# Loading the first expert's first two weight chunks before the expert stage, with bf16 bias rows and a bf16 scatter in three parts

## The chip, the cores and the metric

The kernel runs as one program on one core of a Trainium2 chip. The metric is the device time of one execution in microseconds (us); the time before is 3459.2 us, the median of 3 runs (3454.86 to 3460.97). A lower time is better. Everything is computed in float32 unless bf16 is named.

## What is computed

The input is 256 tokens of width 1024. A first block runs attention, a mixture of 32 experts with 4 chosen for each token, and layer norms; a second block of two layers follows (chunked MLP, gated linear attention, and a lookup of single rows in two large tables, called PEER). Cut to what matters here:

```
def first_block(x, ...):
    y = layer_norm(ALPHA * x + token_mixer(x, w_in, sinks, w_proj_a, w_proj_b, w_out))
    logits = y @ router_w + router_b            # 32 experts
    top_val, top_idx = top_k(logits, 4)
    gates = softmax(top_val)
    for each token and each chosen expert e:
        g = min(y @ w_gate[e] + b_gate[e], 7.0)
        u = clip(y @ w_up[e] + b_up[e], -7.0, 7.0)
        h = g * sigmoid(1.702 * g) * (u + 1.0)
        out += gate * (h @ w_down[e] + b_down[e])
    return layer_norm(ALPHA * y + out)
```

The weights of one expert are three 1024 by 1024 matrices, 12.6 MB, and all 32 experts are read. The second block also has context tokens (`ctx`, 256 by 1024, 1 MB) that are worked on beside the experts.

## The kernel before

**Memory.** Weights come through a ring in SBUF: `sb_ring`, 6 slots of 128 x 4096 floats, 2 MB each. `Ring.load` (issued by L154 from SyncE, here SP) sends one DMA for each chunk of a fixed list, in order, and ahead of each DMA it waits until the slot's former chunk is used up (`chunk_used`). TensorE (PE) waits for a chunk with `Ring.wait` and gives the slot back with `Ring.used`. `sb_arena` is scratch of 16384 columns that is cut anew for each stage; `sb_X` and `sb_H` hold 4 rows of 1024 columns each.

**Front (0 to 316 us).** Attention, the output projection (`w_out`), layer norm and the router. The modulation vectors of the second block are made beside it from 24 chunks `w_mod`. Chunk order at its end: `w_proj_a`, `w_proj_b` x2, `w_out` x2, the last four `w_mod`, then expert 0's chunks `moe0.0` to `moe0.5`. The router's loads (`Router.begin`) and the context tokens (`sb_X<-in_ctx`) go out after the attention; the expert biases (`Router.rest`) go out after the layer norm (`y_ready`). All engines meet at a barrier before the expert stage, and SP comes to it only when these have landed (`Router.loaded`).

**Expert stage (316 to 1315 us).** `expert(p, e)` on PE, for expert e: four short matmuls that put the bias rows into PSUM (L1637, both halves of the columns, gate and up), then `halves` for chunks 0 to 3 (gate and up, L1607), the gather of tokens for a later expert (L1584), transposes of h (L1653), the scatter of the *former* expert's result to the tokens (L1598, `acc[..] += weighT x ye`), the transposes of the weights (L1660), any context work due at this expert (`beside.upto(e)`), and `halves` for chunks 4 and 5 (down projection). `e.c` names chunk c of expert e. VectorE (DVE) makes g, u and h, and ScalarE (ACT) the sigmoid and the copies out of PSUM. Eight chunks for the context work (`context0` to `context7`) stand in the same list, so the ring carries 200 chunks in this stage. SP's order sets the order of all loads: in the stage it runs

```
context.begin(sp)
...
for e in range(NE):
    ring.load(sp, ring.at[f"moe{e}.{PER_EXPERT - 1}"] + 1)
    context.sync(sp, e)
```

Right behind the stage GpSimd (POOL) starts to gather rows of the PEER tables by DMA.

## Time and profile before

| what | value |
|---|---|
| median of 3 runs | 3459.2 us |
| the profiled execution's own time | 3464.24 us |
| its span in the trace | 3462.4 us |
| PE busy, share of the span | 91% |
| DVE, ACT, POOL busy | 54%, 33%, 26% |
| mean DMA rate over the span | 395 GB/s |
| granted TensorE clock, mean | 0.984 |

The profiled execution is 5.0 us above the median. "Busy" is the time in which an engine has an instruction running; for PE the ends of pipelined matmuls are modelled. The DMA rate in slices of 86.6 us shows where transfers are dense and where they pause. Times in rows count from the start of the span.

### The profile page before, as it was taken

What the parts mean: (1) busy time and instruction counts of PE and PEld (TensorE: products, weight loads), DVE (VectorE), ACT (ScalarE), POOL (GpSimd) and SP (SyncE); (2) the same over time, 40 slices, a digit from 0 to 9 for tenths busy, and PEclk for the clock granted to TensorE, in tenths of its full rate; (3) what the DMA queues carried; (4) which work ended last, traced back from release to release, by engine and by line L of the source; (5) the groups of instructions that cost most, each with busy time, mean ns of one, the idle gap of its engine ahead of it and who ended that gap; (6) DMA issues with size and microseconds to landing.
All of it is one profiled execution on the core that took longest, in us unless ns stands there. A gap on an engine that the chain in (4) does not pass through costs nothing. (4 is left out here: it accounts for less than half of the span.)

```text
span 3462.4 us, 33187 instructions
## 1 busy us (share of the span) xinstructions
PE 3144.8 (91%) x10968; PEld 1409.5 (41%) x10968; DVE 1867.1 (54%) x4131; ACT 1131.4 (33%) x3028; POOL 885.8 (26%) x800
## 2 busy tenths in 40 slices
PE   8999999999999997999999888889888998987777
PEld 7574333433334432443345323333332643532222
DVE  7765102111221126776676677667765378667665
ACT  1331111110111113444344444555333434444333
POOL 0000000000000003443444444444442034444332
PEclk9999999999999999999999999999999999999999
DMA  9838999999999999999999999999998479999997
GB/s 404 366 136 341 426 427 428 426 425 428 419 427 428 415 428 405 403 421 414 389 421 416 417 421 419 408 418 412 418 421 343 168 302 420 421 420 421 421 413 329
DMA packets 155665, 1366.42 MB, mean 395 GB/s; under 512 B 18365, under 2 KB 18877, under 8 KB 24162
## 3 DMA queue, kind: packets, MB, share of 16 engines
q0 software_dynamic: 111360, 805.46, 56.4%
q1 hardware_dynamic: 44130, 558.80, 38.7%
q8 instruction: 89, 1.46, 0.2%
q14 instruction: 86, 0.70, 0.1%
HBM read 1363.04 MB, written 1.15 MB: 394 GB/s over the span
## 5 line engine op out<-in xcount | busy, mean ns | idle before, releaser
L3459 PE MATMUL ps<-sb_arena,sb_diag 128*128 128x512 f32 x3072 | 1474.3, 619 | 263.7 <-ACT sb_diag L3438 261.3
L1946 POOL DMA_INDIRECT sb_arena<-in_uv,sb_idx x768 | 865.7, 1127 | 2158.3 <-PE ps L3459 1046.5
L3394 DVE SCALAR_TENSOR_TENSOR sb_arena<-sb_arena,sb_H 128x1024 f32<-128x1024 f32 x768 | 941.1, 1226 | 586.7 <-DMA sb_arena<-in_uv,sb_idx 399.2
L3459 PEld LDWEIGHTS ps<-sb_arena,sb_diag 128*128 128x128 f32 x3072 | 562.6, 194 | 1122.5 <-ACT sb_diag L3438 562.1
L1607 PE MATMUL ps<-sb_ring,sb_arena 128*64 128x512 f32 x3072 | 675.1, 594 | 7.3 <-DMA sb_ring<-in_moe 7.3
L3427 ACT ACTIVATE sb_act<-sb_dots 128x1 f32<-128x1 f32 x768 | 154.8, 202 | 990.7 <-DVE sb_arena L3394 985.5
L1607 PEld LDWEIGHTS ps<-sb_ring,sb_arena 128*64 128x64 f32 x3072 | 214.2, 137 | 446.7 <-issue 430.8
L1808 DVE TENSOR_SCALAR sb_arena<-ps 128x512 f32<-128x512 f32 x32 | 22.1, 692 | 587.1 <-PE ps L1607 571.8
L3438 ACT ACTIVATE sb_diag<-sb_consts,sb_act 128x128 f32<-128x128 f32 x768 | 308.4, 402 | 38.9 <-PE ps L3459 14.1
L3433 ACT ACTIVATE sb_act<-sb_act,sb_wts 128x1 f32<-128x1 f32 x768 | 226.2, 295 | 24.9
L185 PE MATMUL ps<-sb_ring,sb_arena 128*128 128x512 f32 x256 | 111.6, 593 | 2.2 <-DVE sb_arena L889 1.6
L1815 DVE TENSOR_SCALAR sb_arena<-ps 128x512 f32<-128x512 f32 x32 | 22.1, 692 | 158.1 <-PE ps L1607 158.1
L1724 ACT ACTIVATE sb_arena<-sb_arena 128x512 f32<-128x512 f32 x32 | 20.2, 630 | 251.0 <-DVE sb_arena L1808 251.0
L1718 ACT ACTIVATE sb_arena<-ps 128x512 f32<-128x512 f32 x32 | 19.1, 598 | 234.0 <-PE ps L1584 234.0
L1741 ACT ACTIVATE sb_arena<-ps 128x512 f32<-128x512 f32 x32 | 19.1, 598 | 226.9 <-PE ps L1607 226.9
L425 POOL DMA_DIRECT2D mod_rows<-sb_arena x24 | 12.5, 527 | 307.7 <-ACTq L411 307.7
L349 DVE SCALAR_TENSOR_TENSOR sb_arena<-sb_ring,sb_wts,sb_arena 128x2048 f32<-128x2048 f32 x38 | 87.5, 2348 | 1.4 <-DVE sb_arena L349 1.1
L2596 PE MATMUL ps<-sb_ring 128*128 128x512 f32 x192 | 87.7, 600 | 0.0
L185 PE MATMUL ps<-sb_arena,sb_ring 128*128 128x256 f32 x352 | 76.9, 379 | 0.6 <-issue 0.5
L185 PEld LDWEIGHTS ps<-sb_ring,sb_arena 128*128 128x128 f32 x256 | 47.9, 190 | 61.2 <-issue 58.0
L1584 PEld LDWEIGHTS ps<-sb_arena,sb_X 128*128 128x128 f32 x512 | 59.6, 191 | 27.1 <-issue 24.3
L185 PEld LDWEIGHTS ps<-sb_arena,sb_ring 128*128 128x128 f32 x352 | 66.5, 190 | 10.1 <-issue 1.2
(447 smaller groups left out, 2599.0 us busy)
## 6 DMA issues: line engine op xcount, KB each, us to landing
sb_ring<-in_moe SPq DMA_DIRECT2D x192, 2048.0 KB, 16.9
sb_ring<-in_w_mod SPq DMA_DIRECT2D x24, 2048.0 KB, 14.3
sb_ring<-in_w_in SPq DMA_DIRECT2D x10, 2048.0 KB, 14.0
sb_ring<-in_a_w_in SPq DMA_DIRECT2D x8, 2048.0 KB, 15.6
sb_ring<-in_w_q SPq DMA_DIRECT2D x6, 2048.0 KB, 13.0
sb_arena<-in_uv,sb_idx POOLq DMA_INDIRECT x768, 14.7
sb_ring<-in_b_w_in SPq DMA_DIRECT2D x6, 2048.0 KB, 8.8
sb_ring<-in_a_w_out SPq DMA_DIRECT2D x4, 2048.0 KB, 13.9
```

The costliest lines, as they stand in the source:

```text
L185: last = nc.tensor.matmul(out, lhs, rhs, start=i == 0, stop=i == len(pairs) - 1)
L349: ins = nc.vector.scalar_tensor_tensor(out=out, in0=w[:, k, :], scalar=scale, in1=out, op0=ALU.mult, op1=ALU.add)
L1584: last = nc.tensor.matmul(m.ps[:, 7, k * P:(k + 1) * P], m.X[:, t, c:c + P], x.both[:, t, :], start=t == 0, stop=t == TT - 1)
L1607: last = nc.tensor.matmul(m.ps[n * SLOTS:(n + 1) * SLOTS, bank, :], lhs(k + KT // 2 * (c % 2), n), w[:, k, n * 512:(n + 1) * 512], start=f ...
L1808: nc.vector.tensor_scalar(x.g, m.ps[:, 4, :], LIMIT, None, ALU.min).then_inc(M(name("g_ready", p)), 1)
L1946: pool.indirect_dma_start(row_buffer(m, n), None, d[f"uv{layer}"], bass.IndirectOffsetOnAxis(m.idx[:, pair % 2, k:k + 1], 0))\
L2596: last = nc.tensor.matmul(m.ps[:, where[0], :], lhs(k), w[:, k, :], start=k == 0, stop=k == KT - 1)
L3394: nc.vector.scalar_tensor_tensor(out=u, in0=u, scalar=1.0, in1=m.H[:, order[i], :], op0=ALU.mult, op1=ALU.mult, accum_out=m.dots[:, n_ % P ...
L3427: nc.scalar.activation(a, m.dots[:, n_ % PK:n_ % PK + 1], ACT.Gelu_apprx_tanh).then_inc(M("gelu_done"), 1)
L3433: nc.scalar.activation(a, a, ACT.Copy, scale=m.wts[:, pair % 2, k:k + 1]).then_inc(M("act_ready"), 1)
L3438: nc.scalar.activation(m.diag[n_ % DIAGS], m.const("ident"), ACT.Copy, scale=a).then_inc(M("diag_ready"), 1)
L3459: last = nc.tensor.matmul(out[h], m.diag[n_ % DIAGS], uv[b][:, D + h * 512:D + (h + 1) * 512], start=opens, stop=ends)
```

## The change

It has four parts.

1. `moe0.0` and `moe0.1` leave the ring. `first_chunk` loads `moe0.0` in two halves into `sb_H` (rows 0 and 1) and `sb_X` (rows 2 and 3), where the context tokens went; `second_chunk` loads `moe0.1` into the end of the arena (columns 12288 on) once the gates are merged (`merged_ready`). The other chunks keep their order; all slots are turned by two (`(n + 2) % NSLOT`).
2. The context tokens and the two modulation rows for them (`Context.begin`) are loaded in the expert stage, after SP has waited until chunk `moe0.2` is used up, and they stand ahead of the loads of expert 1. DVE waits for three loads (48) in place of two.
3. Gate and up biases are cut into three bf16 parts whose sum is the float32 value: ACT rounds (`bias_upper`, `bias_middle`), POOL subtracts (`bias_less`), and six small DMAs from SBUF to SBUF (`bias_rest`) stack the parts on 96 partitions. PE adds them with four bf16 matmuls of 96 rows in place of four float32 ones of 32 rows.
4. The scatter of all experts but the last uses bf16: DVE makes a 0/1 matrix (`mine`) and three bf16 parts of the result (`split`), ACT multiplies by the gate when it copies the result (`scale=x.gate`), and PE runs twelve bf16 matmuls (`scatter_parts`) in place of four float32 ones.

```
+            router.first_chunk(sp)
+            ring.load(sp, ring.at["w_out"] + 2)
+            sp.wait_ge(M("merged_ready"), KT)
+            router.bias_load(sp)
+            router.second_chunk(sp)
+            ring.load(sp, ring.at["moe0.2"] + 2)
             sp.wait_ge(M("y_ready"), 2 * TT)
             banks.wait_full(sp, mod.where[MOD_END])
             router.rest(sp)
-            ring.load(sp, ring.at["moe0.0"] + PER_EXPERT)
+            router.bias_rest(sp)
+            ring.load(sp, ring.at["moe0.2"] + PER_EXPERT - 2)
             router.loaded(sp)
...
     def begin(self, sp):
         d, M = self.d, self.M
+        self.ring.wait_used(sp, "moe0.2")
+        sp.dma_start(self.m.X[:, 2:4, :], d["ctx"].rearrange("(t p) c -> p t c", p=P)).then_inc(M("context_in"), 16)
...
-            context.begin(sp)
...
             for e in range(NE):
                 ring.load(sp, ring.at[f"moe{e}.{PER_EXPERT - 1}"] + 1)
+                if e == 0:
+                    context.begin(sp)
                 context.sync(sp, e)
...
+            def scatter_parts(count):
+                pe.wait_ge(M("parts_ready"), count)
+                for t in range(TT):
+                    for part in range(3):
+                        for n in range(2):
+                            rows = slice(n * SLOTS, (n + 1) * SLOTS)
+                            last = nc.tensor.matmul(acc[2 * t + n], x.mine[rows, t * P:(t + 1) * P], x.parts[rows, part, :],
...
+                for which in range(2):
+                    for n in range(2):
+                        nc.tensor.matmul(m.ps[n * SLOTS:(n + 1) * SLOTS, 4 + which, :], x.select[0:96, :],
+                                         x.biases[0:96, which, n * 512:(n + 1) * 512], start=True, stop=False, skip_group_check=True)
...
+            def split(e):
+                dve.wait_ge(M("added"), e + 2)
+                dve.wait_ge(M("weighT_ready"), e + 2)
+                step(nc.vector.tensor_scalar(x.mine, x.weighT, 0.0, None, ALU.is_gt))
+                dve.wait_ge(M("ye_ready"), e + 2)
+                step(nc.vector.tensor_copy(x.parts[:, 0, :], x.ye))
+                step(nc.vector.tensor_tensor(x.ye, x.ye, x.parts[:, 0, :], ALU.subtract))
+                step(nc.vector.tensor_copy(x.parts[:, 1, :], x.ye))
+                step(nc.vector.tensor_tensor(x.parts[:, 2, :], x.ye, x.parts[:, 1, :], ALU.subtract), "parts_ready")
```

SP's queue at the end of the front, before the change (in the ring, a slot's number stands in the wait `chunk_used`; here without waits):

```order
L154 DMA sb_ring<-in_w_proj_b 128x4096 x2
L968 DMA sb_H<-in_lns 128x1024 x2
L1358 DMA sb_arena<-in_router_w 128x256
L1358 DMA sb_arena<-in_router_b 1x32
L1359 DMA sb_X<-in_ctx 128x2x1024
L154 DMA sb_ring<-in_w_out 128x4096 x2
L154 DMA sb_ring<-in_w_mod 128x4096 x4
L154 DMA sb_ring<-in_moe 128x4096 x2
L1364 DMA sb_arena<-in_b_gate 32x1024
L1364 DMA sb_arena<-in_b_up 32x1024
L1364 DMA sb_arena<-in_b_down 32x1024
L154 DMA sb_ring<-in_moe 128x4096 x4
```

The same place after the change:

```order
L1390 DMA sb_H<-in_moe 128x2048
L1390 DMA sb_X<-in_moe 128x2048
L154 DMA sb_ring<-in_w_out 128x4096 x2
L1407 DMA sb_w_gate<-in_b_gate 32x1024
L1407 DMA sb_w_gate<-in_b_up 32x1024
L1383 DMA sb_arena<-in_moe 128x4096
L154 DMA sb_ring<-in_w_mod 128x4096 x4
L154 DMA sb_ring<-in_moe 128x4096 x2
L1394 DMA sb_arena<-in_b_down 32x1024
L1402 DMA sb_arena<-sb_arena 32x1024 x2
L1402 DMA sb_arena<-sb_spare 32x1024 x2
L1402 DMA sb_arena<-sb_arena 32x1024 x2
```

Behind these rows only two ring chunks (`moe0.4`, `moe0.5`) go out in the front, where there were four: the six chunks of expert 0 are then all sent, two of them outside the ring.

SP's queue at the start of the expert stage, before the change, with its waits (`ISA` rows clear semaphores):

```order
L1042 DMA sb_H<-mod_rows 128x1024 x2
L1043 DMA sb_stats<-in_a_b_s 128x8
L1044 DMA sb_late_keys<-in_keys 128x128
L1527 ISA x34
L1504 TENSOR_LOAD sb_count [waits late_count]
L1504 ISA x2
L154 DMA sb_ring<-in_moe 128x4096 [waits chunk_used4]
L154 DMA sb_ring<-in_moe 128x4096 [waits chunk_used5]
```

And after the change (`chunk_used0` ahead of the context tokens is the use of `moe0.2`):

```order
L1585 ISA x37
L1563 TENSOR_LOAD sb_count [waits late_count]
L1563 ISA x2
L1053 DMA sb_X<-in_ctx 128x2x1024 [waits chunk_used0]
L1055 DMA sb_H<-mod_rows 128x1024 x2
L1056 DMA sb_stats<-in_a_b_s 128x8
L1057 DMA sb_late_keys<-in_keys 128x128
L154 DMA sb_ring<-in_moe 128x4096 [waits chunk_used4]
L154 DMA sb_ring<-in_moe 128x4096 [waits chunk_used5]
```

What was issued at once now stands behind a wait for a chunk of expert 0, and the first loads of expert 1 stand behind it too; their own slots (4 and 5) are those of the last two `w_mod` chunks.

PE's rows in the middle of one expert, before the change (gather L1584, transposes of h L1653, scatter L1598, transposes of the weights L1660):

```order
L1584 MATMUL ps<-sb_arena,sb_X 128x128 [waits both_picked,bank_free7]
L1584 MATMUL ps<-sb_arena,sb_X 128x128 x7
L1653 MATMUL ps<-sb_consts,sb_arena 128x128 [waits ye_ready,h_ready]
L1653 MATMUL ps<-sb_consts,sb_arena 128x128 x3
L1598 MATMUL ps<-sb_arena 128x512 x4
L1660 MATMUL ps<-sb_consts,sb_arena 128x128 [waits weigh_ready]
L1660 MATMUL ps<-sb_consts,sb_arena 128x128
```

And after it (gather L1644, transposes L1731, scatter L1669, transposes L1738):

```order
L1644 MATMUL ps<-sb_arena,sb_X 128x128 [waits both_picked,bank_free7]
L1644 MATMUL ps<-sb_arena,sb_X 128x128 x7
L1731 MATMUL ps<-sb_consts,sb_arena 128x128 [waits ye_ready,h_ready]
L1731 MATMUL ps<-sb_consts,sb_arena 128x128 x3
L1669 MATMUL ps<-sb_arena 128x512 [waits parts_ready]
L1669 MATMUL ps<-sb_arena 128x512 x11
L1738 MATMUL ps<-sb_consts,sb_arena 128x128 [waits weigh_ready]
L1738 MATMUL ps<-sb_consts,sb_arena 128x128
```

The scatter has twelve matmuls and a wait of its own, for DVE's `split`; before, its four matmuls had none. The four bias matmuls ahead of chunk 0 stay four (L1637 before, L1715 after).

## Rows read from the trace of the kernel before

**Rows 1.** The page, DMA rate in 40 equal slices of the span

```profile
GB/s 404 366 136 341 426 427 428 426 425 428 419 427 428 415 428 405 403 421 414 389 421 416 417 421 419 408 418 412 418 421 343 168 302 420 421 420 421 421 413 329
```

**Rows 2.** Busy time by window: PE, PEld, DVE, ACT, POOL, clock, DMA share, GB/s

```profile
173.00:220.00 47.00, 44.88 (x262) 31.74 (x260) 28.07 (x98) 18.35 (x59) 0.00 (x0) 1.00 0.20 68
268.00:280.00 12.00, 11.39 (x26) 4.96 (x27) 10.76 (x7) 0.00 (x0) 0.00 (x0) 1.00 0.59 199
341.40:1305.10 963.70, 953.09 (x4602) 384.04 (x4602) 169.54 (x393) 126.11 (x209) 3.07 (x4) 1.00 1.00 425
1140.00:1220.00 80.00, 80.00 (x423) 32.09 (x417) 18.20 (x64) 10.09 (x18) 0.00 (x0) 1.00 1.00 418
```

**Rows 3.** Waits in the expert stage: total us, times, longest us

```profile
PE ps L1607 <- DMA sb_ring<-in_moe: 7.3, 8, 1.5
SPq L154 <- PE ps L1607: 746.0, 186, 9.7
```

**Rows 4.** DMA of 341.4 to 1305.1 us: packets, and chunks' median us to landing

```profile
DMA packets 29015, 409.51 MB, mean 425 GB/s; under 512 B 3216, under 2 KB 3216, under 8 KB 4240
...
sb_ring<-in_moe SPq DMA_DIRECT2D x182, 2048.0 KB, 16.9
```

**Rows 5.** Timeline of PE in one expert: start, us, instruction, count

```profile
611.29 1.09 PE L1637 MATMUL ps<-sb_arena 32*64 32x512 f32 x8
612.30 13.95 PE L1607 MATMUL ps<-sb_ring,sb_arena 128*64 128x512 f32 x64
...
628.61 1.99 PE L1598 MATMUL ps<-sb_arena 64*128 64x512 f32 x8
```

**Rows 6.** Timeline of SP, end of the front: start of the first, us, count

```profile
277.50 1.99 SPq L154 DMA_DIRECT2D sb_ring<-in_w_mod  x4
...
303.07 0.42 SPq L1364 DMA_DIRECT2D sb_arena<-in_b_down  x1
305.92 9.32 SPq L154 DMA_DIRECT2D sb_ring<-in_moe  x4
...
327.33 10.63 SPq L154 DMA_DIRECT2D sb_ring<-in_moe  x4
```

**Rows 7.** Us to landing of DMAs issued at 179.57, 297.28, 303.07, 314.91, 327.33

```profile
sb_ring<-in_w_mod SPq DMA_DIRECT2D x1, 2048.0 KB, 7.7
sb_ring<-in_moe SPq DMA_DIRECT2D x1, 2048.0 KB, 15.2
sb_arena<-in_b_down SPq DMA_DIRECT2D x1, 128.0 KB, 11.2
sb_ring<-in_moe SPq DMA_DIRECT2D x1, 2048.0 KB, 18.7
sb_ring<-in_moe SPq DMA_DIRECT2D x1, 2048.0 KB, 14.0
```

**Rows 8.** Timeline of PE, the start of expert 0

```profile
322.62 1.09 PE L1637 MATMUL ps<-sb_arena 32*64 32x512 f32 x8 [0.73 <-issue]
323.64 13.95 PE L1607 MATMUL ps<-sb_ring,sb_arena 128*64 128x512 f32 x64
```

**Rows 9.** Timeline of PE, chunks 3, 4 and 5 of expert 31

```profile
1295.39 3.65 PE L1607 MATMUL ps<-sb_ring,sb_arena 128*64 128x512 f32 x16 [0.53 <-DMA sb_ring<-in_moe]
...
1303.53 7.09 PE L1607 MATMUL ps<-sb_ring,sb_arena 128*64 128x512 f32 x32
```

**Rows 10.** Timeline of DVE, ACT and PE around the layer norm

```profile
268.28 9.14 DVE L349 SCALAR_TENSOR_TENSOR sb_arena<-sb_ring,sb_wts,sb_arena 128x2048 f32<-128x2048 f32 x4
...
284.88 0.20 ACT L958 ACTIVATE sb_stats<-sb_stats 128x1 f32<-128x1 f32 x1 [47.29 <-DVE sb_stats L1894]
...
298.45 0.39 PE L312 MATMUL ps<-sb_w_gl,sb_late_keys 96*2 96x512 bf16 x4
```

**Rows 11.** Groups by line: POOL over the span, DVE in 230 to 1315 us

```profile
L3586 POOL TENSOR_TENSOR sb_X<-sb_X,sb_decay 128x1024 f32<-128x1024 f32 x2 | 3.8, 1888 | 0.0
...
L1813 DVE TENSOR_TENSOR sb_arena<-sb_arena 128x512 f32<-128x512 f32 x32 | 22.2, 693 | 8.1 <-ACT sb_arena L1724 8.1
```

More of the change, by code:

```diff
@@ L516, in _ @@
             router.begin(sp)
-            ring.load(sp, ring.at["moe0.0"] + 2)
+            router.first_chunk(sp)
[4 more added lines that the diff above has]
+            ring.load(sp, ring.at["moe0.2"] + 2)
             sp.wait_ge(M("y_ready"), 2 * TT)
@@ L1049, in sync @@
             self.mod.stored(sp, N_MOD)
+            self.ring.wait_used(sp, "moe0.2")
+            sp.wait_ge(M("added"), 2)
             for i in range(2):
@@ L1260, in vector @@
         yield 0
[L1261 removed]
+        dve.wait_ge(M("context_in"), 48)
         for t in range(TT):
@@ L1343, in __init__ @@
         self.ye = m.part(2560, 512)
-        self.select = m.part(3072, SLOTS)
+        self.select = m.part(12160, SLOTS // 2).bitcast(BF16)
+        self.parts = m.part(5120, 768).bitcast(BF16).rearrange("p (a c) -> p a c", a=3)
+        self.mine = m.part(5888, P).bitcast(BF16)
+        self.gate = m.part(6016, 1)
 class Router:
@@ L1358, in begin, with second_chunk, first_chunk @@
             sp.dma_start(dst, src).then_inc(self.M("router_in"), 16)
-        sp.dma_start(self.m.X[:, 2:4, :], d["ctx"].rearrange("(t p) c -> p t c", p=P)).then_inc(self.M("ctx_in"), 16)
+    def second_chunk(self, sp):
+        sp.dma_start(self.x.second, self.d["moe"][0, 1].rearrange("p (k j) -> p k j", k=KT // 2)).then_inc(self.M("late_first_in"), 16)
+    def first_chunk(self, sp):
+        src = self.d["moe"][0, 0].rearrange("p (k j) -> p k j", k=KT // 2)
+        for dst, ks in ((self.m.H[:, 0:2, :], slice(0, 2)), (self.m.X[:, 2:4, :], slice(2, 4))):
+            sp.dma_start(dst, src[:, ks, :]).then_inc(self.M("late_first_in"), 16)
@@ L1361, in rest, with bias_rest @@
     def rest(self, sp):
         d, x, M = self.d, self.x, self.M
-        for dst, src in ((x.biases[0:NE, :], d["b_gate"]), (x.biases[NE:2 * NE, :], d["b_up"]), (x.b_down[0:NE, :], d["b_down"])):
-            sp.dma_start(dst, src).then_inc(M("biases_in"), 16)
+        sp.dma_start(x.b_down[0:NE, :], d["b_down"]).then_inc(M("biases_in"), 16)
+    def bias_rest(self, eng):
+        eng.wait_ge(self.M("bias_left"), 2)
+        for at, part in enumerate((1, 2, 0)):
+            for which in range(2):
+                eng.dma_start(self.x.biases[at * NE:(at + 1) * NE, which, :],
+                              self.x.bias_parts[part][which * NE:(which + 1) * NE, :]).then_inc(self.M("bias_put"), 16)
@@ L1613, in _, with weights, used @@
             count = None
-            def weights(p, c, e):
+            def weights(p, c, e, first=False):
+                if p == 0 and c == 0 and first:
+                    pe.wait_ge(M("late_first_in"), 48)
+                    return lambda k: (m.H if k < 2 else m.X)[:, k, :]
+                if p == 0 and c == 1 and first:
+                    return lambda k: x.second[:, k, :]
                 if p == 0:
-                    return ring.wait(pe, f"moe{e}.{c}", k=KT // 2)
+                    w = ring.wait(pe, f"moe{e}.{c}", k=KT // 2)
+                    return lambda k: w[:, k, :]
                 pe.wait_ge(M(f"more_in{c}"), 16 * (at(p, e) + 1))
-                return spare[c]
-            def used(p, ins, c, e):
+                return lambda k: spare[c][:, k, :]
+            def used(p, ins, c, e, first=False):
+                if c < 2 and first:
+                    return
                 if p == 0:
@@ L1633, in expert @@
                 context.wait_left(pe, 5)
-                for n in range(2):
-                    for which in range(2):
-                        rows = slice(which * NE, (which + 1) * NE)
-                        nc.tensor.matmul(m.ps[n * SLOTS:(n + 1) * SLOTS, 4 + which, :], x.select[rows, :],
-                                         x.biases[rows, n * 512:(n + 1) * 512], start=True, stop=False, skip_group_check=True)
+                for which in range(2):
+                    for n in range(2):
+                        nc.tensor.matmul(m.ps[n * SLOTS:(n + 1) * SLOTS, 4 + which, :], x.select[0:96, :],
+                                         x.biases[0:96, which, n * 512:(n + 1) * 512], start=True, stop=False, skip_group_check=True)
                 for c in range(4):
                     bank = 4 + c // 2
-                    w = weights(p, c, e)
-                    used(p, halves(bank, c, w, rows_of(p, e), False), c, e)
+                    w = weights(p, c, e, first)
+                    used(p, halves(bank, c, w, rows_of(p, e), False), c, e, first)
                 context.wait_left(pe, 7)
@@ L1654, in expert @@
                 last.then_inc(M(name("h_turned", p)), 1)
-                (down_biases() if p == 0 and first else scatter()).then_inc(M(name("added", p)), 1)
+                (scatter() if p else down_biases() if first else scatter_parts(e)).then_inc(M(name("added", p)), 1)
                 pe.wait_ge(M(name("weigh_ready", p)), at(p, e, 1))
@@ L4174, in program @@
                     front.append((f"context{CONTEXT_AT[e]}", context[CONTEXT_AT[e]], SLOT))
-                front.append((f"moe{e}.{c}", d["moe"][e, c], SLOT))
+                if e or c > 1:
+                    front.append((f"moe{e}.{c}", d["moe"][e, c], SLOT))
         six = 1 + [name for name, _, _ in front].index(f"moe{FIVE_FROM}.0")
-        chunks = [(*chunk, n % NSLOT) for n, chunk in enumerate(front[:six])]
+        chunks = [(*chunk, (n + 2) % NSLOT) for n, chunk in enumerate(front[:six])]
         chunks += [(*chunk, 1 + n % (NSLOT - 1)) for n, chunk in enumerate(front[six:])]
```

76 lines of the change are left out of this document (60 added, 16 removed).

## Prediction, made before the changed kernel ran

> **What bounds the kernel now.** I read the slices of the page first. The DMA rate is 426 GB/s or close to it from the fifth slice on, with a hole in the third (173 to 260 us, 136 GB/s) [rows 1]. The windows then split this: 68 GB/s at 173 to 220 us and 199 at 268 to 280, and in the expert stage 425 over 963.7 us [rows 2]. PE is also busy 953 of those 963.7 us, so one has to decide which of the two sets the pace. Three views say DMA. The best slices stand at 428 and none goes above, whatever PE does beside the experts [rows 1]. A chunk takes 16.9 us from issue to landing [rows 4], but 7.7 us when it goes out alone [rows 7], and 2.097 MB at 428 GB/s is 4.9 us: so nearly three chunks are always under way, and the engines that move them are never out of work. And PE waits for landings, though only for 7.3 us in 8 waits [rows 3]. SP waits 746 us for PE to free slots [rows 3], which looks like a PE limit but is only the ring being full while the queue behind it is deep. So the two are nearly in balance, DMA ahead by a few us, and the end of the stage is the landing of the last chunk plus PE's tail. What counts is the time at which the DMA stream of expert 1 begins, and whether it ever dries up.
>
> **1. First two chunks early.** `first_chunk` (2 MB) takes the place of the context tokens (1 MB) in SP's queue, ahead of `w_out`, in the thin stretch. `second_chunk` and 256 KB of biases go out behind the last gate merge, which is over when DVE turns to its adds at 268.28 us [rows 10], into a stretch at 199 GB/s [rows 2]. With `w_out` ahead of them they need until about 281 (issued at 268.3, 2.8 for a lone DMA, 4.9 for the bytes, some 5 for the rest of `w_out`); the four `w_mod` chunks go out at 277.50 as before [rows 6], so they land about 1 us later (second chunk's remainder). PE needs them 20 us later, so this costs nothing in the front. If that cover were gone, it would be 1 us.
>
> **2. The hole.** Here is the step I trust most. In the new order SP issues nothing between `moe0.5` and the use of `moe0.2`. Before, `moe0.5` landed at 314.91 + 18.7 = 333.6 [rows 7], so `moe0.3`, two chunks ahead of it, near 323.8. It is now `moe0.5` that stands there, and 1 us later by part 1, so the DMA engines fall idle near 325. SP goes on when PE has done three chunks of expert 0. PE begins the biases at 322.62 and the chunks at 323.64 [rows 8]. The bf16 biases take 0.4 us in place of 1.0 (below), and I add 0.8 for a later barrier (part 4): chunks begin at 323.8. One chunk is 13.95/4 = 3.49 us [rows 5, 8], three are 10.5, and the release takes 0.2 (323.64 + 3.49 against the issue at 327.33 [rows 6]): SP issues at 334.5. A lone DMA takes 7.7 - 4.9 = 2.8 us beyond its bytes [rows 7]; the context tokens take 2.45, so they land at 339.7. Then come the rows and `moe1.0`: before, `moe1.0` landed at 327.33 + 14.0 = 341.3 [rows 7], with the same rows between it and `moe0.5`, 7.7 us. So `moe1.0` lands at 347.4, **6.1 us later than before**, although two chunks (9.8 us of DMA time) were taken out ahead of it. The prefetch is eaten by an idle stretch of 334.5 + 2.8 - 325 = 12 us and by 2.45 us of tokens moved into the dense part. PE isn't starved by this at first: expert 0 has its six chunks, 21 us of work with some 6 more between them, so expert 1 starts near 351. Bounds: barrier not later gives 5.3; barrier 1.5 later gives 6.8.
>
> The Trainium skill ("DMA: Bandwidth & Descriptors", section "Anatomy of one DMA — SWDGE (gpsimd) path") fits 2.0 us plus bytes over 436 GB/s for one transfer; that is 6.8 us for a chunk where the row shows 7.7, an estimate that would make the shift 5.3. The row decides, since this is SP's queue and this kernel.
>
> **3. Less work on PE.** Biases: 8 records in 1.09 us for four float32 matmuls on four tiles of the array [rows 5]. After: four bf16 ones with 96 rows; the nearest row, four bf16 matmuls of 96 rows and 512 columns, takes 0.39 [rows 10]. Those used four column groups, these two, so 0.4 to 0.8. Scatter: 1.99 us for four float32 matmuls, in pairs [rows 5]. A float32 matmul of 512 columns here runs as four passes (one chunk: 8 matmuls, pairs, 3.49 us, 0.22 us a pass); twelve bf16 passes in pairs are 6 x 0.22 = 1.3, and 2.6 if pairs don't overlap. Per expert PE saves about 0.6 + 0.7 = 1.3 us, 39 us over 30 experts, between 0 and 1.4 each. None of that shortens a stage that waits for bytes, beyond two places. First the dips: 1140 to 1220 us runs at 418 instead of 427 GB/s [rows 2], where PE's context work lets the queue run low; a faster PE gives back 80 x 9/427 = **1.7 us**. Bounds: 0, if these dips have another cause, and 6.8, if the whole 963.7 us went at 428 instead of 425. Second the tail: chunk 3 of expert 31 is waited for at 1295.39, and the last two chunks begin at 1303.53 [rows 9], with the scatter between; the last chunk landed at 1305.1 (there I ended the window of [rows 2]) while PE reached it at 1307.0, half of 7.09 later. **0.7 us** of scatter come off.
>
> **4. Bias parts.** ACT (two copies of 1024 columns), POOL (two subtractions; a 128x1024 one takes 1.89 us [rows 11]) and ACT again: rows land near 277, so this ends near 283, ahead of ACT's square root at 284.88 [rows 10] and long before `bias_rest`. The Trainium skill ("SBUF — State Buffer", section "Who interferes with whom") says a DVE instruction with two SBUF inputs and a GpSimd one that reads SBUF exclude each other for their whole length; DVE's long adds end at 277.4 [rows 10], so by that rule the layer norm would come at most 1.9 us later; no row here shows such a pair. The six small DMAs go out before 305.92, while SP waits for a slot anyway (0.42 each from about 302.6 on [rows 6]), the last at 305. The bias load issued at 303.07 landed after 11.2 us [rows 7]; the last small one so lands near 316.2. SP came to the barrier behind the chunk of 305.92 + 9.32 = 315.24 [rows 6], so it now comes 1 us later. I take +0.8, already counted in 2.
>
> **5. DVE and ACT per expert.** `split` is five operations, four at about 0.69 [rows 11] and one of half that: 3.1 us, plus a copy on ACT of 0.6. It runs after chunk 5 and must be over before g, which comes after chunk 1 of the next expert, 1.0 + 7.0 us later [rows 5]; with four small operations that build a gather matrix it needs 4.5, an estimate. Cover 3.5 us, cost nothing. PE's new wait for `parts_ready` comes another 7 us after that. Expert 0's g comes a chunk later, hidden by chunk 3. The tokens and their rows arrive near 342.5 and DVE's work on them takes some 5 us (four operations, each twice the 0.69 at most); PE asks for it after chunk 3 of expert 1, past 365.
>
> **Sum.** 6.1 - 1.7 - 0.7 = +3.7 us. On the profiled execution's own 3464.24 that gives 3467.9; it lay 5.0 above the median, and on the median 3459.2 + 3.7 = **3462.9 us**. Behind the stage the gathers of the next one start at the landing of chunk 4 of expert 31 and run dense again, so the shift is passed on one to one. The likeliest case's own range: from 5.3 - 6.8 - 0.7 = -2.2 to 6.8 - 0 - 0 = +6.8, 3457.0 to 3466.0. About 0.2% (6.9 us) is what a measurement of this kernel can tell from no change.
>
> **Rivals.**
> - *The prefetch pays.* If the engines don't fall idle (SP released sooner, or DMA finds other work), `moe1.0` lands at 325.0 + 2.45 + 7.7 = 335.2, 6.1 us earlier; with the other terms -6.1 - 1.7 - 0.7 = -8.5: 3450.7. For it speaks the 4 MB moved into thin stretches; against it the order of SP's queue, in which nothing can pass the wait. A stream that also loses all its dips goes below that. Chance 0.12.
> - *PE was the bound.* Then 39 us of PE work should show, but never beyond the 428 GB/s of the best slices: 6.1 - 6.8 - 0.7 = -1.4, 3457.8. It ends inside the forecast's range; 953 of 963.7 us busy speaks for it, the 8 waits for landings against it. Chance 0.15.
> - *The small bias DMAs hold the barrier.* Six transfers that touch 32 partitions each stand behind `moe0.3`, and a chunk at that place took 15.2 us to land [rows 7]; 305.1 + 15.2 = 320.3, 5 us past today's barrier, moves the whole of expert 0 and the hole by 4.2 beyond the forecast: +7.9, 3467.1. It decides (6.9 against 3.7) from a landing 3.2 us past the forecast's 316.0 on, 319.2. Chance 0.15, since the bias loads beside that chunk landed 4 us faster.
> - *The split reaches PE.* If DVE's chain were 0.5 us too long in 30 experts, +15: 3478. Cover of 3.5 us speaks against it. Chance 0.05.
>
> The forecast has the remaining 0.53. Faster by over 0.2%: the first rival, 0.12, and a little of noise from the second, 0.13 in all. Slower by over 0.2%: the last two and the forecast's upper end, 0.22. Within 0.2%: 0.65. The range reaches to half of the first rival and past the third: 3454 to 3469.
>
> **What would show it.** In the new profile: GB/s low from about 325 to 337 and SP's tokens issued near 334.5 (step 2); the first chunk of expert 1 issued near 337 and landed near 347; PE's longer idle time before L1678, waiting for landings, in sum 30 us or more, with the stage's rate at 427 (step 3); L1715 near 0.4 to 0.8 and L1669 near 1.3 us per expert; the first matmul of expert 0 within a us of 323.6 (step 4). The prediction is wrong if the DMA rate has no gap there, if L1669 comes out near 2.6 and PE isn't seen to wait, or if expert 0 starts after 327.

## The result, and the profile after

The changed kernel takes 3465.76 us, the median of 20 runs (3460.32 to 3472.54); the kernel before took 3458.93 us beside it (20 runs, 3453.55 to 3465.45). The ratio is 1.0019 with a 95% interval of 1.0013 to 1.0024: **6.8 us slower** (4.5 to 8.3). The forecast was 3462.9 us, 3.7 us slower. The profiled execution took 3466.43 us (span 3464.6), 0.7 above its median, where that of before lay 5 above its own; so the two spans differ by only 2.2 us, and the medians count.

The page, DMA rate in 40 slices:

```profile
GB/s 404 366 147 289 427 427 428 427 428 426 426 428 426 423 427 405 407 422 422 396 421 417 420 421 418 402 416 409 419 421 352 161 306 420 418 417 421 421 415 334
```

Two places differ from [rows 1]. The third slice gains (136 to 147): that is the early load of chunk 0. The fourth loses much more, 341 to 289. From the fifth slice on the dips of before (419 and 415) are nearly gone (426 and 423).

Busy time by window (columns as in [rows 2]):

```profile
317.60:326.00 8.40, 6.96 (x34) 6.45 (x34) 1.41 (x8) 2.80 (x6) 2.05 (x4) 0.59 0.67 283
326.00:340.00 14.00, 14.00 (x68) 5.50 (x68) 1.94 (x5) 1.82 (x2) 0.00 (x0) 1.00 0.15 39
350.06:1312.47 962.41, 920.86 (x4592) 378.51 (x4590) 245.35 (x545) 131.10 (x239) 3.07 (x4) 1.00 1.01 426
1140.00:1220.00 80.00, 79.76 (x428) 33.68 (x427) 23.32 (x70) 10.06 (x19) 0.00 (x0) 1.00 1.00 422
```

The second row is the hole: 14 us at 39 GB/s with PE busy all the time. Measured at its edges the hole is longer: 11 GB/s from 323.2 to 338.5 us, since the last bytes of `moe0.5` moved some 2.5 us before it counted as landed (325.72). The first row holds something that I had not forecast: a granted TensorE clock of 0.59, a mean of stretches at 2.4 GHz and at 1.2. SP's timeline and the landings of what it issued:

```profile
306.29 4.22 SPq L154 DMA_DIRECT2D sb_ring<-in_moe  x2
336.95 0.39 SPq L1053 DMA_DIRECT2D sb_X<-in_ctx  x1
...
339.62 1.95 SPq L154 DMA_DIRECT2D sb_ring<-in_moe  x4
```

```profile
sb_X<-in_ctx SPq DMA_DIRECT2D x1, 1024.0 KB, 4.9
...
sb_ring<-in_moe SPq DMA_DIRECT2D x1, 2048.0 KB, 10.4
...
sb_ring<-in_moe SPq DMA_DIRECT2D x182, 2048.0 KB, 20.7
```

The second fence answers to [rows 4, 7]: the tokens of 336.95, the chunk of 339.62 (`moe1.0`, landed 350.06), and the median chunk of the stage (20.7 us where before it was 16.9). SP issues nothing from 310.5 to 336.95, 26 us, then the tokens, their rows and four chunks in a row.

PE's waits in 350 to 1312 us, against 7.3 us in 8 waits in [rows 3]:

```profile
PE ps L1678 <- DMA sb_ring<-in_moe: 38.1, 32, 4.9
```

PE's timeline, start of expert 0 and end of expert 31, which answer to [rows 8, 9]:

```profile
317.62 3.23 PE L1644 MATMUL ps<-sb_arena,sb_X 128*128 128x128 f32 x16 [2.30 <-DVE sb_arena L1862]
321.53 3.73 PE L1644 MATMUL ps<-sb_arena,sb_X 128*128 128x128 f32 x16 [0.69 <-ACT sb_arena L1796]
326.00 0.62 PE L1715 MATMUL ps<-sb_arena 96*64 96x512 bf16 x4 [0.73 <-issue]
326.43 1.91 PE L1678 MATMUL ps<-sb_H,sb_arena 128*64 128x512 f32 x8
...
1302.76 3.65 PE L1678 MATMUL ps<-sb_ring,sb_arena 128*64 128x512 f32 x16 [1.24 <-DMA sb_ring<-in_moe]
...
1308.61 1.47 PE L1669 MATMUL ps<-sb_arena 64*128 64x512 bf16 x12
...
1319.14 1.09 PE L1658 MATMUL ps<-sb_arena 64*128 64x512 f32 x3 [1.67 <-issue]
1324.70 2.92 PE L1658 MATMUL ps<-sb_arena 64*128 64x512 f32 x5 [4.47 <-issue]
```

Before, the same two gathers (L1584 there) took 2.05 us each. The biases take 0.62 us for 1.09, the scatter 1.47 for 1.99. The stage's groups by line, with their counts (L1669 is the scatter, 31 times 12 matmuls; L1892 and L1895 are two of the five operations of `split`, 0.43 and 0.69 us each):

```profile
L1669 PE MATMUL ps<-sb_arena 64*128 64x512 bf16 x372 | 45.5, 378 | 0.0
...
L1895 DVE TENSOR_TENSOR sb_arena<-sb_arena 128x512 bf16<-128x512 f32 x31 | 21.5, 693 | 1.1
...
L1892 DVE CAST sb_arena<-sb_arena 128x512 bf16<-128x512 f32 x31 | 13.3, 427 | 292.3 <-ACT sb_arena L1826 292.3
```

### The profile page after: what moved, and what is told of

The parts are those of the page before. It is cut to its first block and busy times, and to the rows that moved or that the text cites. A ratio compares the mean times of both kernels' runs of the same rounds, so it can differ in the third digit from the quotient of the medians.

```text
span 3464.6 us, 33483 instructions
## 1 busy us (share of the span) xinstructions
PE 3114.8 (90%) x10964; PEld 1407.9 (41%) x10964; DVE 1946.2 (56%) x4286; ACT 1139.6 (33%) x3062; POOL 891.0 (26%) x802
## 3 DMA queue, kind: packets, MB, share of 16 engines
q8 instruction: 90, 1.47, 0.2%
## 5 line engine op out<-in xcount | busy, mean ns | idle before, releaser
L1678 PE MATMUL ps<-sb_ring,sb_arena 128*64 128x512 f32 x3040 | 676.9, 598 | 38.3 <-DMA sb_ring<-in_moe 38.1
L1892 DVE CAST sb_arena<-sb_arena 128x512 bf16<-128x512 f32 x31 | 13.3, 427 | 292.3 <-ACT sb_arena L1826 292.3
L1796 ACT ACTIVATE sb_arena<-ps 128x512 f32<-128x512 f32 x32 | 19.1, 597 | 254.2 <-PE ps L1644 254.2
L1826 ACT ACTIVATE sb_arena<-ps,sb_arena 128x512 f32<-128x512 f32 x31 | 21.3, 687 | 221.4 <-PE ps L1678 221.4
L1644 PEld LDWEIGHTS ps<-sb_arena,sb_X 128*128 128x128 f32 x512 | 62.3, 199 | 27.9 <-issue 24.3
L1644 PE MATMUL ps<-sb_arena,sb_X 128*128 128x128 f32 x512 | 68.5, 289 | 3.0 <-DVE sb_arena L1862 2.3
## 6 DMA issues: line engine op xcount, KB each, us to landing
sb_ring<-in_a_w_in SPq DMA_DIRECT2D x8, 2048.0 KB, 16.9
sb_ring<-in_w_q SPq DMA_DIRECT2D x6, 2048.0 KB, 13.2
```

Source lines behind the costliest of these rows:

```text
L1644: last = nc.tensor.matmul(m.ps[:, 7, k * P:(k + 1) * P], m.X[:, t, c:c + P], x.both[:, t, :], start=t == 0, stop=t == TT - 1)
L1678: last = nc.tensor.matmul(m.ps[n * SLOTS:(n + 1) * SLOTS, bank, :], lhs(k + KT // 2 * (c % 2), n), w(k)[:, n * 512:(n + 1) * 512], start=f ...
```

## The experiments

**How distances are read.** Three marks of the trace split the time up to the second block: the landing of expert 1's first chunk `moe1.0` (what the start costs), the landing of the last chunk `moe31.5` behind it (what the stage costs), and the landing of the 21st gather of the PEER table (the tail, where gathers run dense again). Times are from the traces, and the stage and tail are differences of them; the last columns are medians.

| kernel | `moe1.0` | stage | tail | median us | ratio to before |
|---|---|---|---|---|---|
| before | 341.38 | 963.75 | 64.5 | 3458.93 | |
| before, again | 340.99 | 964.02 | 63.1 | 3457.40 | 0.9996 [0.9987, 1.0005] |
| changed | 350.06 | 962.41 | 65.0 | 3465.76 | 1.0019 [1.0013, 1.0024] |
| changed, again | 348.05 | 962.18 | 63.4 | 3465.76 | 1.0023 [1.0014, 1.0032] |
| four loads | 330.93 | 971.54 | 64.2 | 3456.75 | 0.9991 [0.9982, 1.0000] |
| chunk-0 wait | 342.24 | 962.44 | 64.3 | 3458.95 | 0.9999 [0.9990, 1.0008] |
| both of these | 330.48 | 969.49 | 64.5 | 3456.18 | 0.9990 [0.9981, 0.9999] |
| biases by POOL | 356.38 | 962.38 | 63.5 | 3473.14 | 1.0038 [1.0024, 1.0051] |
| bf16 parts alone | 340.42 | 961.22 | 64.3 | 3458.54 | 0.9996 [0.9986, 1.0005] |
| early load alone | 347.69 | 965.06 | 65.6 | 3467.81 | 1.0021 [1.0012, 1.0030] |
| small biases first | 347.49 | 962.22 | 63.5 | 3465.75 | 1.0017 [1.0008, 1.0026] |
| small biases first, again | 348.14 | 962.50 | 64.1 | 3465.61 | 1.0021 [1.0012, 1.0030] |
| early load alone, four loads | 328.91 | 974.04 | 63.5 | 3460.28 | 1.0002 [0.9993, 1.0011] |
| first, four loads and chunk-0 wait | 330.27 | 969.53 | 64.3 | 3454.39 | 0.9982 [0.9973, 0.9991] |

Each of the twelve experiments was timed beside the kernel before, whose median was then 3460.05, 3459.99, 3459.01 or 3459.84; each ratio is to that one, so kernels are compared by their ratios. Two executions of one kernel differ at `moe1.0` by 0.4 us (before) and 2.0 us (changed).

### Four loads: fill the hole

Two more chunks are sent before the end of the front, and nothing else is changed.

```
-            ring.load(sp, ring.at["moe0.2"] + PER_EXPERT - 2)
+            ring.load(sp, ring.at["moe0.2"] + PER_EXPERT)
```

> The changed kernel, with SP issuing four ring chunks instead of two at the end of the front, so that the first two chunks of expert 1 (their slots are free once the last two w_mod chunks are used) go out ahead of the wait for moe0.2. Theory (the idle DMA stretch of about 14 us behind that wait, and the tokens moved behind it, are what the change costs): two chunks, 9.8 us of DMA work, move into the hole. moe1.0 lands near 330.6 in place of 350.1, a rest of 4 us of idle DMA stays, everything behind it comes 9.8 us earlier: 3456, ratio to before 0.999. Rival (the loss lies in the expert stage's new bf16 and split work or in its later start): the hole closes but the time stays within 2 us of the changed kernel's 3465.8, ratio 1.002.

Measured: 3.3 us faster than before (0 to 6.2), 10 faster than changed by the two ratios, and `moe1.0` at 330.93: the theory's values. Time by window:

```profile
326.00:330.00 4.00, 4.00 (x22) 1.52 (x19) 0.00 (x0) 0.00 (x0) 0.00 (x0) 1.00 1.01 419
330.00:336.00 6.00, 6.00 (x30) 2.33 (x28) 0.90 (x3) 0.17 (x1) 0.00 (x0) 1.00 0.62 265
336.00:350.00 14.00, 14.00 (x60) 6.11 (x58) 7.68 (x11) 2.02 (x5) 0.00 (x0) 0.88 1.01 392
```

The hole moves behind `moe1.1` (landed 335.8; the next chunk at 348.18) and shrinks. The `moe1.0` of this kernel lands 10 us before that of before, but its stage is 8 us longer than that of before, and 9 longer than that of changed. The smaller hole lies in it (65 GB/s from 333.5 to 336.8 us), and so do the tokens and their rows, 2 MB or 4.9 us of transfer that in changed go ahead of `moe1.0`.

### Chunk-0 wait: end the hole sooner

The context tokens' place is held by chunk 0, which is used up 7 us before chunk 2. The instruction that uses it counts for SP:

```
-        self.ring.wait_used(sp, "moe0.2")
+        sp.wait_ge(M("late_first_in"), 49)
...
+                    if c == 0:
+                        ins.then_inc(M("late_first_in"), 1)
```

> The changed kernel, with SP waiting for the use of moe0.0 (which frees the rows of H and X that the tokens and modulation rows are loaded into) in place of moe0.2, two chunks of PE work earlier. Theory (the hole): SP goes on at about 330.0 in place of 336.95, the hole is 7.0 us shorter, and the time falls by as much: 3458.8, ratio to before 1.000. Rival (stage work, not the hole): no change, 3465.8, ratio 1.002. A dose between the changed kernel and the next one.

Measured: 3458.95, as expected. SP goes on at 329.11, where the two executions of changed had 336.95 and 334.84, and `moe1.0` lands 7.8 and 5.8 us sooner than in these:

```profile
329.11 0.39 SPq L1053 DMA_DIRECT2D sb_X<-in_ctx  x1
...
331.76 7.98 SPq L154 DMA_DIRECT2D sb_ring<-in_moe  x4
```

One wait was moved, no byte and no matmul, and the 6.8 us are gone (ratio 0.9999 for 1.0019). The clock fell in the first gather here too (3.52 us), so it isn't what was taken away.

### Both together

> Both edits at once: four ring chunks at the end of the front, and SP waits for moe0.0. Theory (the hole): DMA has work from 277 us on without a pause, 14 us of idle time are gone: 3451.5, ratio to before 0.998. If from here on PE's slots and not DMA's bytes set the pace, the second edit adds less than its 4 us: 3453 to 3456. Rival (stage work): 3465.8.

Measured: 3456.18, a miss against the 3451.5 of the theory and 0.2 us above the alternative's bounds. With the queue full, slots are what is short:

```profile
328.72 0.39 SPq L1053 DMA_DIRECT2D sb_X<-in_ctx  x1
...
335.59 31.37 SPq L154 DMA_DIRECT2D sb_ring<-in_moe  x8
```

The next chunk waits until 335.59 for `moe0.2`'s slot, and those behind it for the chunks that PE uses one by one (`moe1.4` issued at 349.03, landed at 358.82, 8.3 us behind its forerunner). DMA runs at 352 GB/s from 346 to 360 us. The stage is 969.5 us, not 962; 4.9 of the 7.2 us more than in changed are again the tokens and rows that now lie in it, the rest is this wait for slots.

### Biases by POOL: the barrier later

The six small bias loads are issued by POOL instead of SP, ahead of POOL's stores of modulation rows. The waits for chunks 0 and 1 are also moved, from the first matmul of expert 0 into the front (not shown).

```
+                    banks.wait_full(pool, mod.where[MOD_END])
+                    router.bias_rest(pool)
...
-            router.bias_rest(sp)
```

> The changed kernel, with the six small DMAs of the bias parts issued by POOL near 300.6 us in place of SP near 302.4 to 305.7; the first chunks' landings are waited for in the front. Theory: these DMAs landed last at 316.2 and held the barrier; PE then idled 2.3 us and its granted clock fell to 1.2 GHz for the first gathers, so expert 0's chunks started at 326.4 and not 323.0. With the barrier back at 315.4, expert 0 starts 3.0 to 3.4 us earlier, the wait for moe0.2 ends as much earlier and so does all behind it: 3462.6, ratio to before 1.001. Rival: PE's idle time and clock at the barrier stay as they are, because DVE's first operations and not the barrier set them: 3465.8.

Measured: 3473.14, a clear miss in the other direction. PE's timeline:

```profile
323.38 3.79 PE L1646 MATMUL ps<-sb_arena,sb_X 128*128 128x128 f32 x16 [8.09 <-DVE sb_arena L1863]
327.85 3.78 PE L1646 MATMUL ps<-sb_arena,sb_X 128*128 128x128 f32 x16 [0.69 <-ACT sb_arena L1797]
332.37 0.62 PE L1716 MATMUL ps<-sb_arena 96*64 96x512 bf16 x4 [0.73 <-issue]
```

The small bias loads had landed by 315.17, but the stores behind them in POOL's queue landed only at 319.84. PE idled 8.09 us and did both gathers at nearly half speed. Between 319.84 and 323.38 lie 3.5 us, where changed has 1.4 between its last bias landing (316.19) and its first gather; the other 2.1 I can't name. The run still shows how a longer hole is paid for: `moe1.0` comes 6.3 and 8.3 us later than in the two executions of changed, and the ratio rises by 0.0019, 6.6 us. Within the noise the hole's price passes on one to one.

### The bf16 parts alone

The changed kernel with the first two chunks back in the ring behind the others and the context tokens loaded in the front. The core of the edit:

```
-            router.first_chunk(sp)
+            sp.dma_start(m.X[:, 2:4, :], d["ctx"].rearrange("(t p) c -> p t c", p=P)).then_inc(M("ctx_in"), 16)
...
-            router.second_chunk(sp)
-            ring.load(sp, ring.at["moe0.2"] + 2)
+            ring.load(sp, ring.at["moe0.0"] + 2)
```

> The changed kernel with its early load undone: the first expert's first two chunks go back into the ring behind the barrier, and the context tokens and rows are loaded during the front as before; the bf16 bias and scatter parts stay. Theory (the DMA queue sets the pace of the experts' stage): the queue never runs dry, so what is left is the smaller dips and the smaller tail, -1.4 to -1.7 and -0.5 to -0.7, about 2 us below the kernel before: 3457 to 3458, ratio 0.9993 to 0.9995, although the barrier may come later. Rival (TensorE sets the pace, and the early load is no part of it): TensorE does 32 x (0.48 + 0.52) = about 32 us less work and gives back what it had to spare, 5 to 8 us below: 3452 to 3455, ratio 0.998 to 0.999.

Measured: 3458.54, ratio 0.9996, 1.4 us faster than before with an interval of -4.8 to +1.7, so by its time no different from before: nearer to the DMA theory's 2 us than to the rival's 5 to 8, which it only just excludes. The trace is sharper. PE's waits in 360 to 1290 us, and the window of the context work:

```profile
PE ps L1675 <- DMA sb_ring<-in_moe: 31.8, 29, 1.6
```

```profile
1140.00:1220.00 80.00, 80.00 (x446) 34.09 (x444) 27.74 (x89) 11.53 (x23) 0.00 (x0) 1.00 1.01 426
```

PE's saving shows as 31.8 us of waits (6.8 before in the same window). The stage is 2.7 us shorter (961.22 against the two executions of before, mean 963.9), and the dip at 1140 to 1220 is filled: 426 for 418 in [rows 2].

### The early load alone

The kernel before with the early load, float32 biases and scatter kept; the two stages of the last modulation vectors are put in other scratch columns to make room for chunk 1.

```
-            ring.load(sp, ring.at["moe0.0"] + 2)
+            router.first_chunk(sp)
+            ring.load(sp, ring.at["w_out"] + 2)
+            sp.wait_ge(M("merged_ready"), KT)
+            router.second_chunk(sp)
+            ring.load(sp, ring.at["moe0.2"] + 2)
```

> The kernel before with the early load alone: the first two chunks during the front, context tokens and rows behind, fp32 biases and scatter kept. Theory (the hole in the queue is what costs): the barrier is not held by later bias loads, the tokens are issued near 334.4, the third chunk lands about 6 us later than its counterpart before, and nothing of TensorE's work is saved: +6, 3465 to 3467, ratio 1.0016 to 1.0019. Rival (the slower time comes from the bf16 parts, later biases and more instructions): within 1.5 us of before, ratio 0.9996 to 1.0004.

Measured: 3467.81, **7.8 us slower than before** (4.2 to 10.4), a little above the theory's 3465 to 3467 and far from the rival's 1.5 us. The hole is there without any bf16 part, and `moe1.0` lands 6.5 us late:

```profile
304.95 4.80 SPq L154 DMA_DIRECT2D sb_ring<-in_moe  x2
334.58 0.38 SPq L1046 DMA_DIRECT2D sb_X<-in_ctx  x1
...
337.12 11.23 SPq L154 DMA_DIRECT2D sb_ring<-in_moe  x5
```

The two halves add up: +7.8 and -1.4 make +6.4, and the whole change measures +6.8; each half is known to some 3 us only.

### Small biases first: is it the order of the bias loads?

```
+            banks.wait_full(sp, mod.where[MOD_END])
+            router.bias_rest(sp)
             sp.wait_ge(M("y_ready"), 2 * TT)
-            banks.wait_full(sp, mod.where[MOD_END])
             router.rest(sp)
-            router.bias_rest(sp)
```

> The changed kernel with the small bias loads that the barrier waits for issued ahead of the wait for y's projection, and the down bias behind: the same loads in another order. Theory (the extra 2.6 us in the hole come from the last bias load's landing, which leaves TensorE idle for 2.30 us and at a granted clock of 0.59 over the first gathers): the barrier falls near 315.3, the first two gathers take 2.05 us each, the first expert's chunks start at 323.5 to 324.5, tokens are issued near 335, and the time is 2.5 to 3 us below the changed kernel: 3462.5 to 3463.5, ratio to before 1.0010 to 1.0013. Rival (the later start only follows something else, the modulation's store or the front's queue): no change against the changed kernel, 3465.8, ratio 1.0019.

> The changed kernel once more, with nothing edited, beside the next kernel, since a difference of 1 to 3 us is asked for. If the slow first gathers (3.23 and 3.73 us, granted clock 0.59) belong to this kernel, they are seen again, and the tokens are issued near 337; if they belong to that one execution, the gathers take 2.05 us each and the tokens are issued near 334.5 to 335. Time 3465 to 3467, ratio 1.0014 to 1.0024.

> The order of the bias loads changed as before (small loads ahead of the wait for y's projection), timed a second time beside the changed kernel. Theory (earlier barrier, gathers at full clock): 2 to 3 us below the changed kernel of the same job. Rival (the order is worth nothing in the usual execution): within 1.5 us of it.

Measured: 3465.75 and 3465.61, beside 3465.76 for the changed kernel timed with the second. The order is worth nothing that the medians show, and the theory fell on its first step. Whichever bias load is issued last lands last, near 316: the small ones at 316.19 and 315.13 in the two executions of changed, the down bias at 315.71 and 316.57 here. What is left differs from one execution to the next. The gathers of the second execution of the changed kernel, with the window's clock:

```profile
316.93 3.48 PE L1644 MATMUL ps<-sb_arena,sb_X 128*128 128x128 f32 x16 [1.95 <-DVE sb_arena L1862]
321.10 2.05 PE L1644 MATMUL ps<-sb_arena,sb_X 128*128 128x128 f32 x16 [0.69 <-ACT sb_arena L1796]
```

```profile
317.00:321.20 4.20, 3.51 (x17) 3.22 (x17) 0.61 (x3) 2.04 (x4) 2.06 (x4) 0.59 0.99 421
```

and of the second one with small biases first:

```profile
318.23 2.05 PE L1644 MATMUL ps<-sb_arena,sb_X 128*128 128x128 f32 x16 [2.37 <-DVE sb_arena L1862]
321.37 2.05 PE L1644 MATMUL ps<-sb_arena,sb_X 128*128 128x128 f32 x16 [1.08 <-ACT sb_arena L1796]
```

One gather is slow in the first, both were in the execution shown above, none is in the second, though PE had idled longer before it. So of the two cases set out for the second execution of changed neither came whole: the slow gather was seen again, but the tokens went out at 334.84.

### The early load alone, with four loads

> The early load alone, fp32 biases and scatter kept as before, but with four chunk loads issued at the front's end in place of two, so that the queue holds work while TensorE routes and gathers. Theory (the hole in the queue is all that the early load costs, 7.8 us in the early load alone against before): the loss is gone and most of the two chunks' head start stays: 3455 to 3458, ratio 0.9986 to 0.9995, tokens issued near 334, third chunk landed near 331. Rival (without the bf16 parts TensorE has no time to spare and sets the pace once the queue is ahead): within 1.5 us of before, 3459 to 3461, ratio 0.9996 to 1.0004.

Measured: 3460.28, the rival's range; the interval (-2.4 to +3.8 us) also takes in the upper end of the theory's. In the trace `moe1.0` is 12.3 us ahead of the mean of before, but the stage takes 974.0 us, 2.5 more than with the bf16 parts and four loads. A part of the reason stands in its window, where the dip is back:

```profile
1140.00:1220.00 80.00, 80.00 (x430) 33.16 (x428) 19.60 (x70) 11.49 (x21) 0.00 (x0) 1.00 1.00 418
```

The bf16 parts shorten the stage by 2.5 us here and by 2.7 and 2.8 in the two other pairs of the table (before and bf16 parts alone; early load alone and changed). Whether they gain more of the median once the queue is full, this run can't tell.

### First, four loads and chunk-0 wait: the best version

> The changed kernel with bias loads first, four chunk loads at the front's end in place of two, and the first ring load behind that waiting for the first chunk's use instead of the third's. Theory: with the queue never dry, what limits is the use of the slots by TensorE, which starts expert 0 about 1.5 us earlier than with four loads and chunk 0 alone: 1 to 2 us below that kernel's 3456.2: 3454 to 3455.5, ratio 0.9982 to 0.9987. Rival (nothing is left to gain at the start once the queue is full): as that kernel, 3456 to 3457, ratio 0.9989 to 0.9992.

Measured: 3454.39, ratio 0.9982 [0.9973, 0.9991]: 5.6 us (0.2%) faster than before and some 13 faster than changed, as the theory said in size. The reason that was given for it, an earlier start of expert 0, isn't shown: `moe1.0` (330.27) and the stage (969.53) are within 0.3 us of those of both changes without the new bias order (330.48 and 969.49), so the 1.8 us between the two medians may be chance. Beside the bf16 parts alone, timed with it, it is 4.1 us faster (3454.39 for 3458.54), though the intervals of the two ratios just overlap: with the queue kept full the early load seems to pay.

### The kernel before, again

> The kernel before once more, with nothing edited: a second profiled execution, and a comparison of one kernel with itself. All distances of the other runs are taken against one profiled execution of it, which took 5 us more than its median. If that surplus lies in the gathers and the blocks behind them, the first gather is issued at 1301 us here too and the third chunk of before lands at 341.4, both within 0.5 us; if it lies ahead of the first gather, that one comes 1 to 4 us earlier here, and the distances of all runs at the first gather are too small by as much. Ratio 0.9991 to 1.0009.

Measured: 3457.40 us, ratio 0.9996 [0.9987, 1.0005]. The span of its profiled execution is 3455.5 us, 7 less than the first's, yet the chunk stands where it stood:

```profile
327.13 10.63 SPq L154 DMA_DIRECT2D sb_ring<-in_moe  x4
```

It landed 13.9 us later, at 340.99 for 341.38. So the surplus of the first execution lies behind the expert stage, and the distances up to there hold to some 0.4 us. From the 21st gather on the fourteen executions take 2085 to 2093 us with no order by kernel, so 8 us between two spans can come from there alone, and single spans are no measure of these changes.

## Why the prediction was right in kind and too small

**The mechanism holds.** The early load makes a hole in SP's queue and costs time. The chunk-0 wait shows it: it moves one wait, and `moe1.0` comes back by 6.8 us against the mean of the two executions of changed (5.8 and 7.8), and the median by 6.8. That the queue runs dry, and is not merely less full, is the row at 39 GB/s.

**The sum, term by term**, taken as the mean of two profiled executions of changed against two of before:

| term | predicted | measured |
|---|---|---|
| the hole, `moe1.0` | +6.1 | +7.9 (349.06 against 341.19) |
| dips in the stage | -1.7 | -1.6 (962.3 against 963.9) |
| tail | -0.7 | +0.4 (64.2 against 63.8) |
| sum | +3.7 | +6.7 |
| medians | | +6.8 |

That the measured sum meets the medians within 0.1 us is luck: each of its terms moves by 0.2 to 2 us from one execution of a kernel to the next.

- *The start of expert 0* (steps 2 and 4) is the term most mis-sized. The late barrier itself was right: PE's first gather came at 317.62 and 316.93, 0.9 and 0.2 us after before's 316.69, where I had +0.8. What failed is what I left out behind it, the clock. The two gathers together took 6.96 us and 5.53 instead of 4.10. So the chunks began at 326.43 and 324.31 instead of 323.8, 1.6 us late in the mean, and the tokens were issued at 336.95 and 334.84 instead of 334.5. In the first of these executions the sign "the first matmul of expert 0 within a us of 323.6" failed. The rest of the chain was nearly exact: from the tokens' issue to `moe1.0`'s landing I had 12.9 us; the rows say 13.1 and 13.2. In the early load alone, where the clock stayed, my 6.1 plus 0.6 for the float32 biases would be 6.7, and `moe1.0` came 6.5 late. The idle stretch itself was 15.3 us and not 12: I let it begin with the landing of `moe0.5`, but its bytes had ended some 2.5 us before. The shift of `moe1.0` doesn't depend on that.
- *A lone transfer*: the tokens landed 4.9 us after issue, 2.45 of it bytes at 428 GB/s. I had 5.25. The Trainium skill ("DMA: Bandwidth & Descriptors", section "Anatomy of one DMA — SWDGE (gpsimd) path") fits 2.0 us plus bytes over 436 GB/s and would give 2.0 + 2.4 = 4.4, an estimate; the measured value lies between. Its shift of 5.3 for the whole chain is further from the 7.9 than mine.
- *Less work on PE* (step 3, the dips): biases 0.62 us, inside 0.4 to 0.8; scatter 1.47, against 1.3. PE's waits in the stage are 38.1 us for 7.3, the rate 426 to 428 and one dip of 423, as predicted. So the rival in which PE was the bound is out: the bf16 parts alone remove 25 us of PE's busy time between 360 and 1290 us (921.55 to 896.33), and the stage becomes 2.7 us shorter. The -1.7 met its size partly by luck: in the window from which it was priced, 1140 to 1220 us, the rate rose only from 418 to 422; the rest came elsewhere, most of all between 800 and 1000 us (423 to 427).
- *The tail* (step 3): the scatter ahead of the last two chunks did get 0.5 us shorter, but the -0.7 isn't seen. The mean tail of the ten executions with bf16 parts in the table is 64.1 us, of the four without 64.2. The overlap was wrong here: transfers cover PE's tail. In all fourteen executions the first gather of the PEER table is issued 4.0 us before the last chunk lands (1301.12 for 1305.13 before, 1308.48 for 1312.47 after), and three more follow at once. The fifth goes out behind PE's last scatter, 11.7 us after that landing before and 16.5 us in the first execution of changed, where the scatter has a stall (below), and still the 21st lands at nearly the same distance. My own paragraph on the sum had the gathers start at the landing of chunk 4, which leaves nothing for this term.
- *Bias parts and split* (steps 4 and 5): hidden, as said. ACT's square root came at 284.70 for 284.88, and PE waits for DVE nowhere in the stage. The Trainium skill ("SBUF — State Buffer", section "Who interferes with whom") says that a DVE instruction with two SBUF inputs and a GpSimd one that reads SBUF contend. POOL's first subtraction began at 277.88 and DVE's two short ones beside it took 0.69 each as before, so the 1.9 us that the rule allowed didn't come. The rule itself is untested: POOL began only as the long adds ended, and neither of the short ones has two inputs in SBUF.
- *The rival of the small bias loads* had the place right (they hold the barrier) and the size wrong: landed at 316.19 and 315.13, not 320.3. Its +7.9 is nearer to the measured +6.8 than the forecast's +3.7 only by accident.

**What stays open.** Why the clock fell in the first gathers of the changed kernel. PE's idle time ahead of them was 2.30 and 1.95 us there (slow), 2.42 with the chunk-0 wait (first slow), 8.09 with POOL (both slow), but 1.92 with four loads, 1.95 and 2.37 with small biases first and 2.59 with the early load alone, all at 2.05 us each. The idle time alone doesn't sort them. The early load alone had no slow gather and yet is as slow as changed, so the clock isn't what makes the change lose; it explains the gap between 6.1 and the profiled 8.7, and with the medians of small biases first (no slow gather in two executions, same time within 1 us) one can't say that it costs the usual execution anything. In three executions without a slow gather (early load alone with four loads, and the two with four loads and chunk-0 wait) the clock had fallen earlier, ahead of the barrier: their granted clock is 0.50 to 0.57 from 309 to 312 us.

## What to carry to other kernels

A prefetch is worth nothing by itself where the queue that issues it then waits for the slots it has freed: follow the issuing queue to its next wait, and ask when the transfer engines run dry. Here two chunks moved into a thin stretch cost 7.8 us; with two more loads behind them, or (with the bf16 parts) with the wait tied to the buffer that is really needed, they cost nothing that the medians show, and the best version, with both, was some 4 us ahead of the bf16 parts alone. In a stage that waits for bytes, 25 us less work on the compute engine shortened the stage by 2.7 us, in the places where the rate had dipped.

## What the hardware showed that was not expected

- The granted clock fell to a mean of 0.59 (between its levels of 1.2 and 2.4 GHz) right behind a barrier in four of fourteen executions, and gathers of 2.05 us took 3.23 to 3.79. PE had idled 1.95 us or more in all of these, but also where it didn't fall.
- Small loads issued by POOL's queue landed in time, but the four stores behind them landed up to 319.84, where in the other thirteen executions they were in by 313.1 to 315.2.
- In all ten executions with the bf16 scatter the last, float32 scatter (L1658) breaks after three matmuls and goes on 3.0 to 4.5 us later, with no releaser but "issue"; in the four without (both of before among them) its eight run in 1.99 us. The DMA packets of the traces point to the loading of code: in each of the ten one packet of 16 KB of the queue named "instruction" (q8) moves inside the break, and PE goes on 1.4 to 1.6 us after its end (packet 1322.17 to 1323.10, PE at 1324.70 in the first execution of changed). In the four without, such a packet ends 1.6 us ahead of the scatter's first matmul (1310.92 for 1312.48 before), where PE had idled 1.5 to 1.9 us. So the break looks like a wait for instructions that falls at another place in the shorter code; no run changes the length of the code alone to show it. It costs nothing that can be measured in the tail, as DMA is what is waited for there.
